# Four steps of a recurrent layer change engines: a weight as a copy's scale, a decay as an activation's bias, three products on VectorE, and the output gate placed last

## The reference, cut to what matters

```python
b = jnp.cumsum(gc, axis=2)
decay = jnp.exp(jnp.where(causal, b[:, :, :, None] - b[:, :, None], -jnp.inf))
scores = jnp.einsum('bhtsk,bhsk->bhts', qc[:, :, :, None] * decay, kc)
o = (jnp.einsum('bhts,bhsv->bhtv', scores, vc)
     + jnp.einsum('bhtk,bhkv->bhtv', qc * jnp.exp(b), state))
b_last = b[:, :, -1]
state = (jnp.exp(b_last)[..., None] * state
         + jnp.einsum('bhsk,bhsv->bhkv', kc * jnp.exp(b_last[:, :, None] - b), vc))
...
y_rec = rms_norm(o_rec, out_gain) * jax.nn.silu(g_rec.astype(jnp.float32))
```

## Time and profile before

| | |
|---|---|
| median of 3 runs | 1826.55 us (1825.41 to 1828.3) |
| the profiled execution | 1821.69 us, its span 1819.9 us |
| busy, share of the span | PE 91%, DVE 28%, ACT 27%, POOL 11% |
| recurrence | from some 308 to 566 us of the span |
| 345 to 500 us, of 155 | PE 137.34, DVE 107.83, ACT 88.88, POOL 40.02 |

### The profile page before, as it was taken

The page is one execution under the profiler, slowest core; times in us unless marked ns, Lnnn a source line. Parts: engine busy times, 40 slices in busy tenths (PEclk is TensorE's granted clock), DMA queues, the critical chain, the costliest instruction groups (busy, mean ns, idle before and its releaser), DMA issues. The chain is left out here.

```text
span 1819.9 us, 26431 instructions
## 1 busy us (share of the span) xinstructions
PE 1662.2 (91%) x10427; PEld 782.0 (43%) x10427; DVE 503.5 (28%) x1171; ACT 486.0 (27%) x1146; POOL 201.8 (11%) x185
## 2 busy tenths in 40 slices
PE   7999998999888699999679999984999999999996
PEld 3445663455544355555434555541333333333332
DVE  2111300776654223333212333331211111111110
ACT  2254211556552345444200101010111111111111
POOL 0000000322231000000000000011111111111112
PEclk9999998999998899999779999996999999999998
DMA  4513101111036301010093222173899999999983
GB/s 140 173 50 105 47 0 59 49 36 35 29 111 215 100 34 54 29 58 17 18 347 111 81 77 91 41 309 128 344 388 395 406 396 394 406 397 391 400 342 82
DMA packets 83684, 313.21 MB, mean 172 GB/s; under 512 B 20264, under 2 KB 43984, under 8 KB 69984
## 3 DMA queue, kind: packets, MB, share of 16 engines
q1 hardware_dynamic: 61888, 229.34, 33.1%
q10 hardware_dynamic: 9136, 56.95, 7.6%
q0 software_dynamic: 12560, 25.52, 5.4%
HBM read 279.05 MB, written 54.20 MB: 183 GB/s over the span
## 5 line engine op out<-in xcount | busy, mean ns | idle before, releaser
L2256 PE MATMUL ps<-eg,xsT 128*32 128x512 f32 x1152 | 172.0, 600 | 4.5 <-DVE hid L2203 3.2
L1533 PE MATMUL ps<-wg,xt 128*128 128x512 f32 x384 | 174.7, 602 | 0.0
L2256 PE MATMUL ps<-ed,hT 128*32 128x512 f32 x1152 | 169.6, 593 | 4.2 <-DMA fd<-w_expert_down 2.5
L2256 PE MATMUL ps<-eu,xsT 128*32 128x512 f32 x1152 | 169.6, 593 | 3.1 <-DMA fu<-w_expert_up 3.1
L2256 PE MATMUL ps<-fg,xsT 128*32 128x512 f32 x384 | 171.6, 600 | 0.0
L2256 PE MATMUL ps<-fd,hT 128*32 128x512 f32 x384 | 169.3, 594 | 0.0
L2256 PE MATMUL ps<-fu,xsT 128*32 128x512 f32 x384 | 169.3, 594 | 0.0
L2191 DVE TENSOR_TENSOR xsT<-ps,wnT 128x512 f32<-128x512 f32 x48 | 30.9, 686 | 448.7 <-PE ps L2264 448.7
L1986 PE MATMUL ps<-wb,wide 128*128 128x512 f32 x288 | 134.0, 620 | 15.1 <-DVE mg L1884 7.5
L284 PE MATMUL ps<-wbuf,wide 128*128 128x512 f32 (+1 forms) x360 | 144.5, 556 | 3.3 <-DMA wbuf<-w_in 2.8
L2000 PE MATMUL ps<-wo,mgT 128*128 128x512 f32 x288 | 129.3, 603 | 2.8 <-DVE o_lg L1905 2.8
(11 more groups left out here) (338 smaller groups left out, 2195.3 us busy)
## 6 DMA issues: line engine op xcount, KB each, us to landing
eg<-w_expert_gate SPq DMA_DIRECT2D x23, 2048.0 KB, 20.7
eu<-w_expert_up SPq DMA_DIRECT2D x23, 2048.0 KB, 19.8
ed<-w_expert_down SPq DMA_DIRECT2D x23, 2048.0 KB, 19.6
fg<-w_expert_gate ACTq DMA_DIRECT2D x7, 2048.0 KB, 18.1
fu<-w_expert_up ACTq DMA_DIRECT2D x7, 2048.0 KB, 15.8
fd<-w_expert_down ACTq DMA_DIRECT2D x7, 2048.0 KB, 15.5
gt<-g_dram SPq DMA_DIRECT2D x9, 1024.0 KB, 5.6
wbuf<-w_in SPq DMA_DIRECT2D x7, 1024.0 KB, 7.4
```

What stands on the lines that cost most here:

```text
L1533: mm = pe.matmul(ps[2 + (n + j) % 2][:, :], x, wg[j][:, k, :], start=(k == 0), stop=(k == KC - 1))
L2256: last = pe.matmul(bank[c, :], rows[:, c], mine if q < 3 else other, start=start, stop=stop)
```

## The change

GpSimd's part in tiles 0 to 7 goes, and its steps are placed elsewhere:

- The norm's weights are loaded as one value per partition (`gain` [128, 1]). By then `y` is transposed, with the value dimension on the partitions, so ACT applies them as the `scale` of its copy from `psy` to `mixT`. GpSimd's product L622 goes.
- `dl` needs no subtraction: ACT computes exp(-b + b_last) from `bT` itself, one activation per head, since the bias is one value per partition and head. The sample tile, whose ends are every 16 frames, keeps the subtraction, now on DVE in tile 7 (`sample_decay`).
- `qe`, `kd` and the gate's product become `query`, `key` and `gated` on DVE: behind levels 4 and 5, and at the tile's end. `gated` reads `psh` in PSUM directly, so `z` and its copy go, and PE's next `hg` waits for `gated` (`s_sg`) and not for ACT's sigmoid (`s_he`).
- ACT's output gate stands behind all levels, between the copies of the first and the last far level to `M`.
- In the sample tile `gated` stands between the state products of heads 0 and 1, and GpSimd's four `vm` products follow one another.

The diff, without the deleted declarations and GpSimd's deleted code, which the quoted functions above show:

```diff
         near = m.sb("near", [P, H, STRIP])
-        gain = m.sb("gain", [P, P])
+        gain = m.sb("gain", [P, 1])
         s_const = m.sem("r_const")
...
             sp.dma_start(dd[:, :, :], A.c_masks.rearrange("p (l n) -> p l n", n=HW)).then_inc(s_const, 16)
-            sp.dma_start(gain[:, :], A.hgrn_out_norm[0].partition_broadcast(P)).then_inc(s_const, 16)
+            with nc.allow_non_contiguous_dma(reason="one gain per partition"):
+                sp.dma_start(gain[:, :], A.hgrn_out_norm[0].rearrange("(p o) -> p o", o=1)).then_inc(s_const, 16)
             sp.dma_start(stream[:, :], A.c_stream).then_inc(s_const, 16)
...
                                    stream[:, :].unsqueeze(2).to_broadcast([P, STREAMS, P]), ALU.mult).then_inc(s_vm, 1)
-                if h == 0:
-                    output_gate(ST)
             pool.wait_ge(s_zw, 16)
...
                 act.activation(eb[:, :], T.bT[:, i, :], ACT.Exp).then_inc(s_eb, 1)
-                act.wait_ge(s_dl, i + 2)
-                act.activation(dl[:, :], dl[:, :], ACT.Exp).then_inc(s_dle, 1)
+                if isinstance(i, int) and i == ST:
+                    act.wait_ge(s_dl, 2)
+                    act.activation(dl[:, :], dl[:, :], ACT.Exp).then_inc(s_dle, 1)
+                else:
+                    act.wait_ge(s_kd, i + 1)
+                    for h in range(H):
+                        last = act.activation(dl[:, h * P:(h + 1) * P], T.bT[:, i, h * P:(h + 1) * P], ACT.Exp, scale=-1.0,
+                                              bias=T.bT[:, i, (h + 1) * P - 1:(h + 1) * P])
+                    last.then_inc(s_dle, 1)
                 if later(i, 1):
...
                 act.wait_ge(s_yt, i + 1)
-                act.copy(T.mixT[:, i, 0:HW], psy[:, :]).then_inc(s_mx, 1)
+                act.activation(T.mixT[:, i, 0:HW], psy[:, :], ACT.Copy, scale=gain[:, 0:1]).then_inc(s_mx, 1)
...
                 act.activation(hge, psh[:, :], ACT.Exp, scale=-1.0)
-                act.copy(z, psh[:, :])
                 act.drain()
...
                 act.drain().then_inc(s_ma, 1)
+                output_gate(i)
                 act.wait_ge(s_lv, i * NL + NL)
...
                         mixed(i - 1)
-                    if l == 5:
-                        output_gate(i)
                 if last:
...
             decays(0, 0)
+            act.wait_ge(s_const, RCONST)
             rolled(act, tile)
...
             dve.drain()
-            bh = blocks(T.bT[:, 0, :], P)
-            dve.tensor_tensor(blocks(dl[:, :], P), bh[:, :, P - 1:P].to_broadcast([P, H, P]), bh, ALU.subtract).then_inc(s_dl, 1)
             dve.wait_ge(s_const, RCONST)
...
             dve.memset(tick[:, :], 0.0).then_inc(s_mk, 1)
-            dve.wait_ge(s_eb, 1)
-            dve.tensor_tensor(qe[:, 0, :], T.qT[:, 0, :], eb[:, :], ALU.mult).then_inc(s_qe, 1)
-            dve.wait_ge(s_dle, 2)
-            dve.wait_ge(s_kt, 1)
-            dve.tensor_tensor(kd[:, :], T.kT[:, 0, :], dl[:, :], ALU.mult).then_inc(s_kd, 1)
+
+            def query(i, n):
+                dve.wait_ge(s_eb, i + 1)
+                if later(i, 2):
+                    dve.wait_ge(s_o, i - 1)
+                dve.tensor_tensor(qe[:, n, :], T.qT[:, i, :], eb[:, :], ALU.mult).then_inc(s_qe, 1)
+
+            def key(i):
+                dve.wait_ge(s_dle, i + 2)
+                dve.wait_ge(s_kt, i + 1)
+                dve.tensor_tensor(kd[:, :], T.kT[:, i, :], dl[:, :], ALU.mult).then_inc(s_kd, 1)
+
+            def sample_decay():
+                bh = blocks(T.bT[:, ST, :], SLEN)
+                dve.tensor_tensor(blocks(dl[:, :], SLEN), bh[:, :, SLEN - 1:SLEN].to_broadcast([P, HW // SLEN, SLEN]),
+                                  bh, ALU.subtract).then_inc(s_dl, 1)
+
+            def gated(i):
+                dve.wait_ge(s_he, i + 1)
+                dve.tensor_tensor(sg, hge, psh[:, :], ALU.mult).then_inc(s_sg, 1)
+
+            query(0, 0)
+            key(0)
...
             def outputs(i):
-                dve.wait_ge(s_sg, i + 1)
                 dve.wait_ge(s_r, i + 1)
...
                         outputs(i - 1)
+                    if l == 2 and isinstance(i, int) and i == PT - 1:
+                        sample_decay()
+                    if l == 4 and not last:
+                        query(i + 1, 1 - n)
+                    if l == 5:
+                        key(i + 1)
                 if last:
...
                     difference(i + 1, 0)
+                    gated(i)
...
             tile(ST, 0)
-            for h in range(2):
-                streams(h)
+            streams(0)
+            gated(ST)
+            streams(1)
             square_sums(ST)
...
                     if later(i, 1):
-                        pe.wait_ge(s_he, i)
+                        pe.wait_ge(s_sg, i)
                 mm = pe.matmul(psh[:, :], XK(b, k), whg[:, k, :], start=(k == 0), stop=(k == KC - 1))
```

More of the change, by code:

```diff
@@ L520, in recur @@
         gb = T.mixT[:, 4, HW:]
-        z = T.mixT[:, 8, HW:]
         s_xt = [m.sem(f"r_xt{n}") for n in range(2)]
@@ L605, in _ @@
             pool.wait_ge(s_const, RCONST)
[L607 to L632, removed]
-                output_gate(i)
-            rolled(pool, tile)
             pool.wait_ge(s_o, PT)
```

## The result

The changed kernel takes 1803.53 us (four runs, 1799.48 to 1807.6), the kernel before 1826.78 us beside it: ratio 0.987, 95% interval 0.984 to 0.990. It is faster, as forecast, but by 23.3 us and not 15.8; the time lies 2.5 us under the forecast's own range (1806 to 1815) and 1.5 under the wider one (1805 to 1820). Run again later, in five runs, it has 1804.82 against 1823.7: 0.990 (0.988 to 0.992), 18.9 us. (1823.7 is the median of the kernel before's eight fast runs there; a ninth, slow one took 4694.29 us and is left out.)

A forecast was written before the change was run, and what follows sets the result against it. TensorE nearly bounds the recurrence, idling for VectorE's operands, which GpSimd's products delay. Tiles -20.9, sample_decay +0.3, collision +3.4, gate product +0.65, clock +0.8 sum to -15.8 us: 1826.55 becomes 1810.8, range 1806 to 1815 (wider 1805 to 1820).

The forecast's parts named there:

- Slots 4 and 5: Steady tile: TensorE's waits of 0.99 and 0.30 us for VectorE's operands go once GpSimd's products no longer run beside them.
- Slot 7: Steady tile, level 6: TensorE's wait of 1.59 us goes, with ACT's gate moved behind the exponentials and z's copy gone.
- Slot 6: Steady tile: a new TensorE wait of about 0.2 us, behind ACT's scaled copy and exponentials and VectorE's operands.
- behind slot 7: Tile's end: ACT's last copy to M and VectorE's wait for the gate hold nobody; spare 1.45, 3.6 and 3.8 us.
- The collision in the sample tile: GpSimd's four consecutive vm products delay VectorE's levels 2 and 3, alternating with it: cost 3.4 us, between 0 and 5.3.
- the clock in the sample tile: Eight gate matmuls in the sample tile: more TensorE idle time may keep the 1.2 GHz level longer, 0.8 us, 0 to 3.
- the start at nothing: Start of tile 0, waiting for constants: gain's shorter DMA was costed at 0 us, from -0.5 to 0.5.
- Everything after the recurrence ... moves as a whole: Attention, merge and experts start behind the recurrence's last instructions and only shift with it; no gain or cost of their own.
- the second (new waits): Steady tiles: ACT becomes the bound and new waits eat half the gain, tiles of 24.4, 1821 us; chance 0.09.
- the fourth (gate late): Tile's end: ACT's late gate makes M's last copy hold TensorE; slower, 1836 us at 5 us late; chance 0.05.
- the third (not GpSimd's doing): Steady tiles: VectorE's long instructions don't come from GpSimd, 25.4 a tile, net -3, 1823.5 us; chance 0.07.
- the first: Sample tile costs more as GpSimd keeps the port and TensorE the low clock: net -9.6, 1817 us; chance 0.12.

## Why the prediction was wrong

The forecast of -15.8 us and the measured -23.3 lie 7.5 apart. By the profiles 4.2 of that lie in the recurrence, in the steps below; 2.3 lie in the phases behind it, and 1 is the difference between the profiled executions and the medians. These last 3.3 are not shown to be the change's. In the second set of runs the gain is 18.9 us, which from 1826.55 gives 1807.7, inside the range; but in both pairs of profiles the recurrence gained more than the 15.8 (19.9 and 19.0).

**Right.** *Slots 4 and 5* lose their waits, and for the reason given: DVE's products go back to 0.69 and 0.42, and GpSimd's reads alone bring waits back. *Slot 7* loses its wait as forecast, but the reason was in part wrong: the step named ACT's gate, which "held its exponentials", first, and the gate put back costs nothing, while GpSimd's products bring 1.05 us back. That the number came out there is partly luck. *Slot 6* gets the forecast wait: 0.25 against 0.2. The copy with its scale cost 0.10 more, 0.69 against 0.59; I had taken 0.08. The 93 ns that the Trainium skill (ScalarE: Activation LUTs, What ACT_TABLE_LOAD costs) gives agree with it. The tile is 23.00, forecast 22.9. The four exponentials took 1.26 us (1.2) and were covered; nothing waited behind slot 7. Seven tiles gave 20.3 us, forecast 20.9 less the 0.3 of `sample_decay`: 20.6; tile 7, which has it, took 23.05 and so hardly felt it.

*The collision in the sample tile* was forecast at 3.4 us. Level 2's operands end 3.65 later (11.32 us after slot 0 against 7.67), and `y` is ready 3.18 later (15.46 against 12.28). The transposes start 3.86 later; the 0.68 more is PE's, told below. The engines alternate: DVE's three instructions end at 509.52, 511.55 and 513.59, one behind each product, and GpSimd's four products only at 515.34, so its queue did not keep DVE out. The output gate's product cost 0.52, forecast 0.65: from DVE's first block of states to attention's first matmul it is 13.94 against 13.42.

**Wrong: the clock in the sample tile.** The step was "More idle time may keep the 1.2 GHz level longer: 0.8, between 0 and 3". The eight matmuls behind the transposes gave 1.69 us back instead, and slow matmuls ahead of them cost 0.68: a net gain of 1.0, 1.8 us off. Before, PE's idle time stood at three places up to the transposes:

```profile
532.66 0.46 PE L978 MATMUL ps<-qk 128*32 128x32 f32 x32 [0.78 <-DVEq L823]
...
535.49 0.46 PE L978 MATMUL ps<-qk 128*32 128x32 f32 x32 [0.47 <-DVEq L823]
537.23 0.66 PE L943 MATMUL ps<-eye,sq 128*128 128x128 f32 x4 [1.28 <-DVE sq L851]
```

After, it is more, but earlier: one wait of 4.43 us before slot 3. The clock fell there, and the slow stretch covered the four gate matmuls behind it (3.78 us). Those lay beside DVE's next steps: `y` was ready at some 517.7, and PE came to transpose it at 518.46, so the slow matmuls cost some 0.7 us and not 1.8. When the eight matmuls ran, the clock was back, for 3.60 instead of 5.29. The changed kernel's second profile has the four matmuls faster:

```profile
516.99 3.15 PE L923 MATMUL ps<-whg,wide 128*128 128x512 f32 x4
```

There PE came to the transposes as `y` was ready, 15.52 us after slot 0 and not 16.19, and the sample tile took 43.34 and not 44.02. I had excluded a gain without a reason: which matmuls lie in the slow stretch can change, and I had asked only how long it is. The profiles with this wait have 3.60 to 3.84 for the eight matmuls, both profiles of before 5.29, and with late `vm` products, where the clock stayed at 1.00, they take 3.60; no run changed the clock alone, so the account of it is read, not tested.

**Wrong: the start at nothing.** The step was "gain's DMA keeps 128 rows, shorter, and I cost it at 0, from -0.5 to 0.5". It gave 2.4 us at the cast in the profiled pair (2.1 at slot 0, since the recurrence began 0.3 later) and 1.9 in the second pair. Of the nine profiles in which the cast waits behind the 0.5 KB load, eight have it 5.88 to 7.00 us after DVE's first instruction and one, with the gate early, 9.73; the two of before have 8.51 and 8.68. I had looked at the last load, the stream, and called it unchanged. What counts is when it lands, and it is issued behind 64 KB or 0.5 KB. That the small load is the cause is likely by these profiles, not shown: the run that put the 64 KB back (10.09) is hardly later than the one exception.

**Wrong: "Everything after the recurrence ... moves as a whole".** The phases behind gave another 2.3 us in the profiled pair, and 3.9 in the second, whose two profiles are from different chips. As they vary by themselves by 1 to 4 us, part of that is chance; that an earlier or differently timed recurrence shifts attention and merge by some 2 us is not excluded and stays open. The range had nothing for it.

The sum: -15.8, tiles +0.4, start and tile 0 -2.4, sample tile -2.2, makes the -19.9 measured where the change is (terms rounded). The later phases make it 22.3, and the medians differ by 1 us more. Of the rivals, the second (new waits) and the fourth (gate late) show no trace, and the third (not GpSimd's doing) fell with the experiments; the first had the right place, the sample tile, with the wrong sign.

## What to carry to other kernels

Where VectorE multiplies two SBUF tiles on the path that feeds TensorE, look at what GpSimd reads at that moment, at each place: moving its work off can be worth as much as DVE's instructions shrink, where PE waits for them, and a bundle of GpSimd products left elsewhere (here 4.9 to 5.6 us) costs the same way. When idle time moves, ask not only how long the low clock lasts but which matmuls it then covers and whether they wait for something anyway. Where an engine waits for several loads, look at the loads issued ahead of the last one too, and let it wait only for what it needs (here the masks).

## What was not expected of the hardware

GpSimd lost little in these collisions: three products beside DVE took 3.66 us (1.22 each, against the 1.27 of the earlier trace rows), four large ones 8.26 against 7.46 alone; only `kd`, 1.72, lost 0.45. DVE paid: 0.4 to 1.1 us an instruction beside small products, and 1.5 to 1.7, most of a product of 1.90, beside large ones.

A load of 0.5 KB in 128 rows in place of one of 64 KB let the next load on that queue, 4 KB, land in 4.1 to 4.9 us in the two profiles of the changed kernel, where it took 6.6 and 6.9; in one other kernel with the small load it took 7.9. The masks' own load took 4.2 to 4.4 throughout.
